# Down projection of a SwiGLU layer: nine instead of seven of its 22 tiles as 2x2 block products

## The reference

```python
def _swiglu(x, w_gate, w_up, w_down):
    return (jax.nn.silu(x @ w_gate) * (x @ w_up)) @ w_down      # hidden width 5632

x = _layer_norm(DEEPNORM_ALPHA * x + _swiglu(x, w_gate, w_up, w_down), ln2_g, ln2_b)
```

## Time and profile before

| | before |
|---|---|
| median of 3 runs | 926.62 us (926.18 to 927.84) |
| the profiled execution | 926.27 us, span 924.5 us |
| PE, PEld busy | 917.8 us (99%), 767.2 us (83%) |
| DVE busy | 742.3 us (80%) |
| ACT, POOL busy | 530.2 us (57%), 81.2 us (9%) |
| down | from 686.6 us of the span to 916.6, 1014 matmuls |
| behind it, to the end of the span | 7.9 us |

### The profile page before, as it was taken

How to read it: one execution, slowest core, us unless ns; L and a number is a source line. 1 busy time by engine, 2 the same in 40 slices (tenths; PEclk the granted TensorE clock), 3 DMA queues, 4 the chain that set the end, 5 groups by cost and what they waited for, 6 DMA issues and landing times.

```text
span 924.5 us, 11752 instructions
## 1 busy us (share of the span) xinstructions
PE 917.8 (99%) x4376; PEld 767.2 (83%) x4376; DVE 742.3 (80%) x985; ACT 530.2 (57%) x755; POOL 81.2 (9%) x86
## 2 busy tenths in 40 slices
PE   9999999999999999999999999999999999999997
PEld 8999988888878888878888888888888888888885
DVE  6778566578688888888888888888857987999677
ACT  5686765454455656565656656565554555456550
POOL 0105540000400001020100101000000000000000
PEclk9999999999999999999999999999999999999999
DMA  9844324584907677586867677586588656365542
GB/s 364 326 158 146 129 91 160 205 319 146 399 23 274 184 249 232 185 265 194 275 198 267 178 254 220 195 270 196 178 302 323 244 212 245 121 230 223 228 137 91
DMA packets 55560, 199.61 MB, mean 216 GB/s; under 512 B 5584, under 2 KB 11728, under 8 KB 44240
## 3 DMA queue, kind: packets, MB, share of 16 engines
q1 hardware_dynamic: 55472, 198.86, 61.9%
q0 software_dynamic: 32, 0.00, 0.0%
HBM read 188.88 MB, written 9.96 MB: 215 GB/s over the span
## 4 chain that ended last, share of the span: by engine, by line
PE 97%; DVE 2%; ACT 1%; issue 0%; DVEq 0%; ACTq 0%
PE acc L2127 22%; PE acc L2154 21%; PE acc L1898 9%; PE acc L2109 9%; PE tp L2127 7%; PE tp L2109 6%; PE acc L1836 5%; PE tp L2154 4%; PE acc L1757 4%; PE acc L2035 2%; PE acc L1870 1%; PE tp L1949 1%; PE tp L2073 1%; PE tp L1884 1%; PE tp L1962 1%; PE tp L1746 0%
## 5 line engine op out<-in xcount | busy, mean ns | idle before, releaser
L2127 PE MATMUL acc<-w_hi,act_t 128*128 128x512 f32 x600 | 191.6, 390 | 0.1
L1121 ACT ACTIVATE w_hi<-raw 128x512 fp32r<-128x512 f32 (+1 forms) x154 | 114.5, 781 | 94.4 <-PE acc L2154 84.8
L2154 PE MATMUL acc<-w_hi,hid_t 128*128 128x512 f32 x504 | 161.0, 389 | 0.0
L1548 DVE TENSOR_TENSOR w_lo<-raw,w_hi 128x512 fp32r<-128x512 f32 (+1 forms) x154 | 131.5, 880 | 33.1 <-ACT w_hi L1121 33.1
L1477 DVE TENSOR_TENSOR w_lo<-raw,w_hi 128x1024 fp32r<-128x1024 f32 x104 | 125.2, 1216 | 23.5 <-ACT w_hi L1072 22.9
L1072 ACT ACTIVATE w_hi<-raw 128x1024 fp32r<-128x1024 f32 x100 | 104.9, 1055 | 52.3 <-PE acc L2127 37.5
L2127 PEld LDWEIGHTS acc<-w_hi,act_t 128*128 128x128 f32 x600 | 112.6, 188 | 25.3 <-issue 1.0
L2127 PE MATMUL acc<-w_lo,act_t 128*128 128x512 f32 x300 | 116.8, 389 | 0.0
L2154 PEld LDWEIGHTS acc<-w_hi,hid_t 128*128 128x128 f32 x504 | 94.6, 188 | 19.6
L1057 ACT ACTIVATE w_hi<-raw 128x1024 fp32r<-128x1024 f32 x63 | 66.7, 1058 | 63.9 <-PE acc L2127 36.8
L1467 DVE TENSOR_TENSOR w_lo<-raw,w_hi 128x1024 fp32r<-128x1024 f32 x63 | 77.2, 1226 | 29.7 <-ACT w_hi L1057 29.5
(11 more groups left out here) (287 smaller groups left out, 1766.9 us busy)
## 6 DMA issues: line engine op xcount, KB each, us to landing
raw<-in_w_pairs SPq DMA_DIRECT2D x136, 512.0 KB, 4.9
raw<-in_w_down SPq DMA_DIRECT2D x44, 1024.0 KB, 5.9
raw<-in_w_out SPq DMA_DIRECT2D x16, 1024.0 KB, 4.9
third_raw<-in_w_pairs SPq DMA_DIRECT2D x36, 256.0 KB, 4.7
raw<-in_w_gu SPq DMA_DIRECT2D x8, 1024.0 KB, 10.3
raw<-in_x_w SPq DMA_DIRECT2D x14, 552.0 KB, 7.4
hid_blocks<-local SPq DMA_DIRECT2D x11, 512.0 KB, 5.0
turned<-hid_blocks SPq DMA_DIRECT2D x44, 128.0 KB, 4.3
```

The source lines that it names most:

```text
L1121: act.activation(unit_parts(u)[0], block_of(b, block, width), ACT.Copy).then_inc(down_hi_done, 1)
L1548: dve.tensor_tensor(lo_, block_of(b, block, width), hi_, ALU.subtract).then_inc(down_lo_done, 1)
L2127: last = pe.matmul(out[:, t, :], act_t[:, k0 + m, x, t * P:(t + 1) * P], part[:, cols][:, m * GC:(m + 1) * GC], start=False, stop=(end and ...
L2154: last = pe.matmul(bank, lhs(x), part[:, cols * GC:(cols + 1) * GC], start=(first == u and (cols, x) == (0, 0) and part is hi_), stop=(end ...
```

## The change

Nine tiles (0, 2, ... 16) are quads, not seven; tiles 14 and 16 are the new ones. REST has the tiles 18 to 21 in both pairs. In each pair the 63 products stand in one row and the halves of the nine odd tiles are dealt evenly among them (pair 0: two halves ahead of all). This gives 126 products and 52 halves, 178 units; FIRST_REST is (81, 85, 170, 174), where it was (71, 75, 142, 150).

The factors of tiles 14 and 16 are not made early from the turned tile. GpSimd makes them from the parts in `hid_t` once the gate factors' memory is free (`late_sums`: per tile five instructions, then two for the low parts), ACT makes their high parts behind the units 14 and 34 (`late_high`, two instructions each), and PE waits for them at the first product of the two quads. `LAST_TURN` goes from 5 to 8 and `LAST_HID` from 13 to 28, and some of PE's waits ahead of down are put later.

```diff
-DOWN_QUADS = (0, 2, 4, 6, 8, 10, 12)
+DOWN_QUADS = (0, 2, 4, 6, 8, 10, 12, 14, 16)
+EARLY_QUADS = 7
+LATE_QUADS = len(DOWN_QUADS) - EARLY_QUADS
...
-REST = ((18, 19), (20, 21)), ((14, 15), (16, 17), (18, 19), (20, 21))
+REST = ((18, 19), (20, 21)), ((18, 19), (20, 21))
...
+        products = [(tile, "product", q, n) for q, tile in enumerate(DOWN_QUADS) for n in range(PRODUCTS)]
+        halves = [(tile, "plain", tile, col) for tile in (1, 3, 5, 7, 9, 11, 13, 15, 17) for col in range(2)]
+        steps = halves[:2] if pair == 0 else []
+        halves = halves[len(steps):]
+        for n, half in enumerate(halves):
+            cut = [len(products) * m // len(halves) for m in (n, n + 1)]
+            steps += products[cut[0]:cut[1]] + [half]
...
-LAST_TURN = 5
-LAST_HID = 13
+LAST_TURN = 8
+LAST_HID = 28
+LATE_HIGH = (14, 34)
...
+            def late_high(n):
+
+                act.wait_ge(late_step, 5 * (n + 1))
+                act.activation(late_t[:, n, 0, :, :], late_sum[:, n, 1, :, :], ACT.Copy)
+                act.activation(late_s1(n, 0), late_hid[:, 0, P:S], ACT.Copy).then_inc(late_hi_done, 1)
...
+                if u in LATE_HIGH:
+                    late_high(LATE_HIGH.index(u))
...
+            def late_sums(n):
+
+                i = 2 * DOWN_QUADS[EARLY_QUADS + n]
+                c11, c12, c21, c22 = (late_hid[:, c, t * P:(t + 1) * P] for t in range(TOK) for c in range(2))
+                s2, s3, s4 = (late_sum[:, n, 1, m, :] for m in (S2, S3, S4))
+                done = 5 * n
+                pool.tensor_tensor(late_hid[:], hid_t[:, i:i + 2, 0, :], hid_t[:, i:i + 2, 1, :], ALU.add)\
+                    .then_inc(late_step, 1)
...
+                pool.wait_ge(late_hi_done, n + 1)
+                pool.tensor_tensor(late_t[:, n, 1, :, :], late_sum[:, n, 1, :, :], late_t[:, n, 0, :, :], ALU.subtract)
+                pool.tensor_tensor(late_s1(n, 1), late_hid[:, 0, P:S], late_s1(n, 0), ALU.subtract).then_inc(s_lo, 1)
+
+            pool.wait_ge(*used_step(V_OF[PAIRS - 1, "third", P4]))
+            pool.wait_ge(ffn_lo, PAIRS - 2)
+            for n in range(LATE_QUADS):
+                if n > 0:
+                    pool.wait_ge(s_lo, EARLY_QUADS + n)
+                late_sums(n)
...
                 if u == 0:
+                    pe.wait_ge(ffn_lo, PAIRS - 2)
+                    pe.wait_ge(ffn_hid, TILES - 1)
+                if u == QUAD_FIRST[0]:
+                    pe.wait_ge(s_lo, EARLY_QUADS)
+                    pe.wait_ge(ffn_hid, TILES)
+                if u in QUAD_FIRST[EARLY_QUADS:]:
+                    pe.wait_ge(s_lo, QUAD_FIRST.index(u) + 1)
+                if u == FIRST_REST[0]:
                     pe.wait_ge(ffn_lo, PAIRS - 1)
-                    pe.wait_ge(ffn_hid, TILES - 1)
-                    pe.wait_ge(s_lo, len(DOWN_QUADS))
-                if u == 4:
-                    pe.wait_ge(ffn_hid, TILES)
```

More of the change, by code:

```diff
@@ L202, in down_plan @@
     for pair in range(DOWN_PAIRS):
[L203 to L217, removed]
+        products = [(tile, "product", q, n) for q, tile in enumerate(DOWN_QUADS) for n in range(PRODUCTS)]
[5 more added lines that the diff above has]
+            steps += products[cut[0]:cut[1]] + [half]
+        held = {}
+        for tile, kind, x, y in steps:
+            if tile not in held:
+                held[tile] = slot(pair, "both", (tile,))
+            place = (Q_BLOCK[y], 1) if kind == "product" else (2 * y, 2)
+            units.append((pair, held[tile]) + place + ((kind, x, y),))
         for col in range(2):
@@ L256 @@
                      for pair in range(DOWN_PAIRS))
+QUAD_FIRST = tuple(min(u for u, unit in enumerate(DOWN_UNITS) if unit[4][:2] == ("product", q))
+                   for q in range(len(DOWN_QUADS)))
 PAIR_FIRST = (0, FIRST_REST[1] + 2 * len(REST[0]))
@@ L295, in layer_kernel @@
         xn = sb("xn", [P, TOK, D])
-        sb("s_rest", [P, len(DOWN_QUADS) * 2 * 3 * P + 2 * 4 * 2 * P - TOK * D])
+        sb("s_rest", [P, EARLY_QUADS * 2 * 3 * P + 2 * 4 * 2 * P - TOK * D])
         s_gate = nc.alloc_sbuf_tensor_at("s_gate", [P, 2, 4, 2, P], F32R, offset=base_x)
-        s_t = nc.alloc_sbuf_tensor_at("s_t", [P, len(DOWN_QUADS), 2, 3, P], F32R, offset=base_x + 2 * 4 * 2 * P * 4)
-        s_sum = nc.alloc_sbuf_tensor_at("s_sum", [P, len(DOWN_QUADS), 2, 3, P], F32, offset=base_x + 2 * 4 * 2 * P * 4)
+        s_t = nc.alloc_sbuf_tensor_at("s_t", [P, EARLY_QUADS, 2, 3, P], F32R, offset=base_x + 2 * 4 * 2 * P * 4)
+        s_sum = nc.alloc_sbuf_tensor_at("s_sum", [P, EARLY_QUADS, 2, 3, P], F32, offset=base_x + 2 * 4 * 2 * P * 4)
+        late_t = nc.alloc_sbuf_tensor_at("late_t", [P, LATE_QUADS, 2, 3, P], F32R, offset=base_x)
+        late_sum = nc.alloc_sbuf_tensor_at("late_sum", [P, LATE_QUADS, 2, 3, P], F32, offset=base_x)
+        late_hid = nc.alloc_sbuf_tensor_at("late_hid", [P, 2, S], F32, offset=base_x + LATE_QUADS * 2 * 3 * P * 4)
         ident = sb("ident", [P, P])
@@ L496, in layer_kernel @@
         s_lo = sem("s_lo")
+        late_step = sem("late_step")
+        late_hi_done = sem("late_hi_done")
         x1_stored = sem("x1_stored")
@@ L533, in hid_of, with late_s1 @@
             return tiles[:, :, :, x, :]
+        def late_s1(n, x):
+            return hid_t[:, 2 * DOWN_QUADS[EARLY_QUADS + n], x, P:S]
         def hid_blocks(p, x):
@@ L1105, in _ @@
                     hid_hi(PAIRS - 2)
-                if (kind, n) == ("first", HID_AT) and 2 <= p < len(DOWN_QUADS) + 2:
+                if (kind, n) == ("first", HID_AT) and 2 <= p < EARLY_QUADS + 2:
                     q = p - 2
@@ L1731, in _ @@
             for p in range(1, PAIRS):
-                if 0 <= p - 2 < len(DOWN_QUADS):
+                if 0 <= p - 2 < EARLY_QUADS:
                     factor_low(p - 2)
-                if p - 1 < len(DOWN_QUADS):
+                if p - 1 < EARLY_QUADS:
                     factor_sums(p - 1)
+            def late_sums(n):
[5 more added lines that the diff above has]
+                    .then_inc(late_step, 1)
+                pool.wait_ge(late_step, done + 1)
+                pool.tensor_tensor(s3, c11, c21, ALU.subtract).then_inc(late_step, 1)
+                pool.wait_ge(late_step, done + 2)
+                pool.tensor_tensor(c21, c21, c22, ALU.subtract).then_inc(late_step, 1)
+                pool.wait_ge(late_step, done + 3)
+                pool.tensor_tensor(s2, c21, c11, ALU.subtract).then_inc(late_step, 1)
+                pool.wait_ge(late_step, done + 4)
+                pool.tensor_tensor(s4, c12, s2, ALU.add).then_inc(late_step, 1)
+                pool.wait_ge(late_hi_done, n + 1)
[7 more added lines that the diff above has]
+                late_sums(n)
             pool.wait_ge(xt_full, TOK * CHUNKS)
@@ L2157, in multiply, with factor @@
                 return last
+            def factor(q, x, n):
+                return s_t[:, q, x, n, :] if q < EARLY_QUADS else late_t[:, q - EARLY_QUADS, x, n, :]
             def product_unit(u):
```

8 lines of the change are left out of this document (4 added, 4 removed).

## The result

The kernel after takes 938.75 us (median; 934.82 to 940.01), the kernel before 926.72 in the same comparison: a ratio of 1.0123, interval 1.0112 to 1.0135. The prediction said 932.0 and at most 934.2. The sign and most of the steps hold, the time doesn't: the change costs 12.0 us, over twice what was forecast.

A forecast was written before the change was run, and what follows sets the result against it. PE's matmuls were taken to bound down, with DVE second and 2.3 us of slack at the end. End +2.4, start +0.9 and clock +2.4 gave +5.7 on 926.27, so 932.0 us (chance 0.60); range 928.3 to 934.2.

The forecast's parts named there:

- The matmuls: Down on PE: two more quads in two pairs save 3 matmuls each, twelve in all, -2.7 us.
- The mix at nothing: Down's even row of quads and plain tiles: DVE needs 8.9 us per 10.2 of PE, so no cost.
- The start, +0.9: Start of pair 0 in down: PE waits 0.35 us at unit 15, GpSimd slows DVE; +0.9 us, from 0.3 to 1.8.
- The round trip at nothing: Later loads of `turned` for tiles 20 and 21: 0 us, with 0.5 as upper bound.
- The end, +2.4: End of span: eight folds make DVE 4.8 us later, so DVE ends last, +2.4 us against the kernel before.
- The clock, +2.4: Six matmuls with diag run at the lower clock after PE's 5.3 us pause: +2.4 us, bounds 0 and 2.8.
- Rival B: The clock stays up for the matmuls with diag: +3.3 us, 929.6; chance 0.17.
- The late factors at nothing: PE's waits for the late factors at units 63 and 72, 70 us into down, cost nothing.
- The range: 928.3 (B, start at lower bound) to 934.2 (A, start and clock at upper bounds); 0.2 chance outside.
- C: Rival: the end hides the folds in DVE's pauses before unit 173, so PE's saving stands, 924.5; chance 0.08.
- E: Rival: DVE is short in down's mix and PE waits 2 to 4 us more, 934 to 936; chance 0.07.
- D: Rival: the end costs about what PE saves and the clock stays, 926 to 928; chance 0.08.

The follow-up runs named there:

- experiment 7: Experiment 1's kernel with tiles 15 and 17 back in REST of pair 1, same number of matmuls: 924.56 us, ratio 0.9981 to the kernel before.
- experiment 3: Experiment 1's kernel plus one unused GpSimd instruction once DVE has finished twelve units: 933.38 us with a subtraction of 128x384, 933.13 us with a memset (one run).
- experiment 2: The kernel after with ACT's high factors of tile 16 made behind unit 54, not 34: 933.30 us, ratio 1.0074 to the kernel before.
- experiment 6: Pair 1's folds behind units 171 to 173, not 173 to 176: 937.08 us on the kernel after, 929.87 us on experiment 1's kernel.
- experiment 1: The kernel after with ACT making tile 14's high factors ahead of down and tile 16's behind down's first unit: 932.17 us, ratio 1.0061 to the kernel before.
- experiment 5: Experiment 1's kernel plus ten unused matmuls in PE's pause before diag: 929.53 us, ratio 1.0033 to the kernel before.
- experiment 4: Experiment 1's kernel plus many unused GpSimd subtractions of 128x384: 20 started by ACT's progress, 936.33 us; 24 by DVE's, 939.55 us (one run each).

## Why the prediction was right and wrong

- **The matmuls**: right. PE has twelve fewer (4364, before 4376), and experiment 7 collects their worth.
- **The mix at nothing**: right. PE waits for a low part once besides the stop, by 0.2 us. But at the start of pair 0 DVE has no pause at all from 698 to 724, and GpSimd needed one.
- **The start, +0.9**: 0.5 measured. The wait at unit 15 came where it was put, near 705, and is 0.33 us (705.37 - 704.81 - 0.23), forecast 0.35. The 0.5 us for two GpSimd instructions ahead of it were too much: the one that came was held off and cost DVE nothing. Where they are let in, 0.26 us for each of the seven is too little: DVE's instruction takes 1.52 us beside one of 128x384 (experiment 3), 1.77 beside one of 128x512 and 0.95 beside one of 128x128 (experiment 2), against 0.69, some 3.2 us for the seven.
- **The round trip at nothing**: right. SP issues the loads of `turned` at 707.59, and ACT takes them at 715.50 without a wait.
- **The end, +2.4**: right to 0.1, by the steps of the prediction, shifted by what had come before; so is PE's wait for bank 3 (1.38 us, forecast 1.5). Experiment 6 adds what the step missed: even without the folds in the way DVE's 8.18 us would have set the end.
- **The clock, +2.4**: 2.65 measured. On experiment 1's kernel, where it is 5.08 - 2.81 = 2.3, experiment 5 gives it back. Rival B falls.
- **The late factors at nothing**: this is the step that failed, and by itself it accounts for what the forecast was short (938.75 - 932.0 = 6.75 us). The prediction looked at PE's waits for these factors, 70 us into down, and found them free. It did not walk the wait that stands earlier: ACT's for GpSimd's sums of tile 16 at unit 34, with every high part of down queued behind it. By the durations used there it was free as well: two low parts and five sums, at 1.8 and 1.3 us each, are some 10 us from 702.4, and ACT comes to it at 722.57. What turned it was the duration: "each of the seven costs DVE about 0.26 us" took a GpSimd instruction beside DVE to last 1.0 to 1.8 us, from rows of gate and up, where DVE pauses again and again (1.07 us just before the stretch of the earlier trace rows), and carried this over to one where DVE has no pause and no operand in PSUM. The instruction took 22.7 us. Missing were 4.8 us of stop and 2.1 us of half clock. Experiments 1 and 2 take the wait away in two ways, and the time falls by 6.6 and 5.5 us.
- **The range**: its lower end doesn't follow from its words. B with the start at its lower bound is 926.27 + 2.4 + 0.3 = 929.0, and not 928.3; with either end the measured 938.75 lies outside.

The prediction cited the Trainium skill (SBUF — State Buffer, Who interferes with whom), whose rule is that of a VectorE instruction with two SBUF inputs and a GpSimd instruction that reads SBUF, one blocks entirely, and that issue order decides which. I set it aside for the row's 0.26 us. The traces show both sides of it: GpSimd is the one blocked in the long instructions, and DVE the one that waits (1.52 instead of 0.69 us) when GpSimd is let in. The Trainium skill also says there that a GpSimd instruction that only writes doesn't contend with such a VectorE instruction; the one memset, 0.42 us beside DVE's usual 0.68, agrees, at a moment when the subtraction was let in as well. That a block may outlast 34 of DVE's instructions is not said in that section.

**The rivals.** C (the end hides the folds) was priced at 924.5 with a threshold of 5.0 us of slack. Experiment 6 shows that hiding the folds is not enough, and experiment 7 comes to 924.56 with another order, by chance the same number. E expected several waits for low parts from a DVE short of time: refuted by experiment 1. D and the rest didn't occur.

Open: why a GpSimd instruction is let in up to 3.7 us behind DVE's last pause and not from 4.3 us on (experiment 4), and why the kernel after spreads over 934.82 to 940.01 where experiment 1 spreads over 1.2 us. Two kernels with the stop have a trace, this one and the first of experiment 6, and the stop is the same in both (GpSimd 22.73 us, DVE's pause 6.52). The run of 934.82 had a mean granted clock of 0.996, as experiment 1's runs had, whose trace has one stretch at half clock, against 0.993 to 0.995 for the others, whose trace has two; so one of the two was perhaps missing in it, but it has no trace.

## What to carry to other kernels

Walk every wait that an edit puts in an in-order engine's queue, and price it by the queue behind it: here the free waits were PE's, and the dear one was ACT's. Here the same GpSimd instruction took 1.3 us or over 20 beside a VectorE that didn't pause; take its results from a stretch with pauses, or give the consumer tens of us, and test a probe at the moment in question: 2 us earlier gave another answer. And when work is taken from the last stage, check both sides of its overlap: the folds in front of the last ring unit, and the matmuls that cover the normalization behind it.

## What the runs showed of the hardware

- A GpSimd subtraction of 128x384 with both operands in SBUF takes 1.0 us, or up to 23.9 us beside a DVE that runs tensor_tensor back to back. In 44 trials eight took 11.9 us or more; each ended 0.87 to 0.89 us after DVE paused, and a pause of 0.03 us was enough. All 11 that were held off started at least 4.29 us behind DVE's last pause or lengthened instruction, the 29 let in at most 3.7 us behind it (experiment 4).
- When it is let in, DVE pays: 1.52 instead of 0.69 us for one instruction of 512. Beside a GpSimd instruction of 128x512 it was 1.77, beside one of 128x128 0.95.
- PE's granted clock fell 2.0 us after PE stopped in mid-down (727.4, then 0.73 over 729 to 730), and some 4.3 us after its last product at the end (923.2, then 0.72 over 927 to 928); before the change it was 2.2 to 2.4 us. It was back at full 4.2 us after the matmuls had resumed at 732.1. The Trainium skill (TensorE: Matmul & The Clock Gate, Part 1) has the low clock as the state that activity lifts, and both the half-clock matmuls after the stop and the ten of experiment 5 agree.
